# 352 instead of 384 columns for TensorE's U products, and the last 32 dense tokens from gathered rows

## What is computed

```python
comb = (sv[:, :, 0, :, None] + sv[:, :, 1, None, :]).reshape(T, PEER_HEADS, K * K)
cs, ci = lax.top_k(comb, K)
idx = ia * PEER_NKEYS + ib
g = jax.nn.softmax(cs, axis=-1)
a = jnp.einsum('td,thkd->thk', xb, u_tab[eb])          # pre-activation: h . U row
w = gb * jax.nn.gelu(a, approximate=False)
return jnp.einsum('thk,thkd->td', w, v_tab[eb])        # weighted sum of V rows
```

## Time and profile before

| | |
|---|---|
| Runs | 1338.08, 1338.53, 1338.57 us; median 1338.53 |
| Profiled execution | span 1336.4 us, by which it is known here; the runs' median is 2.1 us above it |
| TensorE | busy 1314.3 us (98%) |
| VectorE | busy 1160.9 us (87%) |
| ScalarE | busy 656.3 us (49%) |
| GpSimd | busy 573.2 us (43%) |
| DMA | 384.51 MB, mean 288 GB/s |
| Granted TensorE clock | 0.999 of full speed |

### The profile page before, as it was taken

One profiled execution on the slowest core, in us unless ns is written; L12 is line 12 of the kernel. 1 busy time (PEld: TensorE's weight loads), 2 busy tenths in 40 slices (PEclk: granted clock), 3 DMA queues, 4 the chain that ended last, 5 costly groups with the idle time before them and its releaser, 6 DMA issues.

```text
span 1336.4 us, 23193 instructions
## 1 busy us (share of the span) xinstructions
PE 1314.3 (98%) x7713; PEld 712.3 (53%) x7713; DVE 1160.9 (87%) x2288; ACT 656.3 (49%) x926; POOL 573.2 (43%) x347
## 2 busy tenths in 40 slices
PE   6999999999999999999999999999999999999997
PEld 3554555456666666666655555555544444444444
DVE  8866399999988999999778888899998889888887
ACT  5652555556676767676543333333343334333342
POOL 4741233435643434343336666667653433222202
PEclk9999999999999999999999999999999999999999
DMA  7231322336677999999999999999999999999952
GB/s 297 96 111 64 107 83 85 104 96 188 192 252 238 321 386 381 364 359 379 401 332 357 363 362 362 355 402 390 382 368 384 391 388 388 382 370 371 374 181 105
DMA packets 148796, 384.51 MB, mean 288 GB/s; under 512 B 11776, under 2 KB 71424, under 8 KB 146560
## 3 DMA queue, kind: packets, MB, share of 16 engines
q1 hardware_dynamic: 111872, 249.54, 52.8%
q0 software_dynamic: 36864, 134.23, 25.8%
HBM read 340.74 MB, written 42.99 MB: 287 GB/s over the span
## 4 chain that ended last, share of the span: by engine, by line
PE 98%; DVE 1%; ACT 1%; DMA 0%; issue 0%; DVEq 0%; ACTq 0%
PE bank L696 39%; PE bank L684 16%; PE bank L686 16%; PE bank L685 16%; PE bank L961 2%; PE bank L905 2%; PE bank L903 2%; PE bank L711 2%; PE bank L852 1%; PE bank L610 1%; PE bank L810 1%; DVE stats L1381 0%; PE bank L757 0%; PE bank L734 0%; PE bank L746 0%; PE bank L624 0%
## 5 line engine op out<-in xcount | busy, mean ns | idle before, releaser
L696 PE MATMUL bank<-cut,area 128*128 128x512 f16 x2208 | 482.9, 380 | 0.0
L684 PE MATMUL bank<-hT,cut 128*128 128x384 f16 (+1 forms) x1216 | 407.2, 335 | 0.0
L685 PE MATMUL bank<-hT,cut 128*128 128x384 f16 (+1 forms) x1216 | 407.2, 335 | 0.0
L686 PE MATMUL bank<-hT,cut 128*128 128x384 f16 (+1 forms) x1216 | 407.1, 335 | 0.0
L992 ACT ACTIVATE cut<-raw 128x1024 f16<-128x1024 f32 x246 | 255.7, 1053 | 198.7 <-PE bank L696 130.8
L696 PEld LDWEIGHTS bank<-cut,area 128*128 128x128 f16 x2208 | 215.8, 98 | 256.7
L1358 DVE SCALAR_TENSOR_TENSOR cut<-raw,cut 128x1024 f16<-128x1024 f32 x198 | 250.6, 1267 | 60.6 <-ACT cut L992 59.2
L1207 ACT ACTIVATE gelu_out<-bank 128x384 f32<-128x384 f32 x120 | 58.9, 491 | 252.9 <-PE bank L686 252.9
L592 POOL DMA_INDIRECT ple_sb<-u_rows_dram,expert_id x64 | 112.9, 1764 | 134.0 <-DVE dots_now L1708 101.5
L582 POOL TENSOR_TENSOR cut<-raw,cut 128x1024 f16<-128x1024 f32 x48 | 108.0, 2250 | 139.9 <-ACT cut L1002 139.9
L686 PEld LDWEIGHTS bank<-hT,cut 128*128 128x128 f16 x1216 | 118.8, 98 | 89.0
(11 more groups left out here) (207 smaller groups left out, 1556.7 us busy)
## 6 DMA issues: line engine op xcount, KB each, us to landing
raw<-tiles_dram SPq DMA_DIRECT2D x298, 512.0 KB, 6.5
gates_scratch<-area SPq DMA_DIRECT2D x12, 2048.0 KB, 11.6
area<-gates_scratch SPq DMA_DIRECT2D x32, 768.0 KB, 9.6
gelu_scratch<-gelu_out SPq DMA_DIRECT2D x80, 192.0 KB, 5.1
area<-gelu_scratch SPq DMA_DIRECT2D x20, 768.0 KB, 11.3
norm_rows<-norms_dram SPq DMA_DIRECT2D x3, 1024.0 KB, 7.6
hn<-x_dram SPq DMA_DIRECT2D x4, 512.0 KB, 5.2
out_dram<-hn SPq DMA_DIRECT2D x3, 512.0 KB, 2.6
```

Source lines behind the costliest of these rows:

```text
L684: nc.tensor.matmul(dst, w[0], hT[:, 0, k, 0:width], start=(k == 0), stop=False)
L685: nc.tensor.matmul(dst, w[0], hT[:, 1, k, 0:width], start=False, stop=False)
L686: last = nc.tensor.matmul(dst, w[1], hT[:, 0, k, 0:width], start=False, stop=(k == KD - 1))
L696: mm = nc.tensor.matmul(bank[:, 2 * tt + h, :], lhs(a)[:, tt * P:(tt + 1) * P], cut[:, t.slot, b, h * HALF:(h + 1) * HALF], start=(first a ...
```

## The change

The last 32 of the 384 dense tokens (`TOK` tokens of the third tile, `TU` = 352 up) get their U pre-activations no longer from TensorE. They have 32 x 128 picks; laid over 128 partitions (four groups of 32 tokens with 32 picks each) these are `EXTRA` = 32 gathered blocks of 128 U rows, and as many dots on VectorE with `extra_h`, a copy of h of these 32 tokens in each of the four groups. VectorE transposes the dots in 32 x 32 blocks (`turn_extra`), ScalarE applies the GeLU, VectorE multiplies with the gates (`weigh_extra`) and writes the result into the rows from which the one-hot matrices of these tokens take their values. So the gate matrix holds gate times GeLU for them, and the GeLU columns of these tokens are set to 1. V products stay 384 wide.

The extra 32 dots come first, in the gate stage, so the sparse tokens' dots and sums move back: there the stage's last 16 dots are theirs (as before, one gather and one dot a tile); then 8 in the kept tiles and 24, 24, 24 and now 32 in four eights; the fifth eight has 26 sums and the late part 102 instead of 80, 10 or 11 for an eight. VectorE's loops over the gate stage, the eights and the late part are written out, and the copies `dots_now` and `sparse_w_now`, which the loops needed, are gone.

```diff
+TU = TD - TOK
+EXTRA = TOK * HK // P
+EXTRA_TILE, EXTRA_AT = TU // P, TU % P
 KEPT_DOTS = 8
-EIGHT_DOTS = (24, 24, 24)
-EIGHT_SUMS = (26, 22)
+EIGHT_DOTS = (24, 24, 24, 32)
+EIGHT_SUMS = (26,)
+LATE_SUMS = (10, 10, 10, 10, 10, 10, 10, 10, 11, 11)
...
@@ SP
             sp.dma_start(subkeys_sb, subkeys).then_inc(subkeys_in, 16)
+            sp.wait_ge(norm_done, 2 * TT - 1)
+            for g in range(P // TOK):
+                sp.dma_start(extra_h[g * TOK:(g + 1) * TOK, :],
+                             hn[EXTRA_AT:EXTRA_AT + TOK, EXTRA_TILE, :]).then_inc(extra_h_in, 16)
             for n in range(T_Q + RING, T_Q + LOAD_AHEAD):
...
@@ GpSimd
+            for n, (table, ids, i) in enumerate([*((u_rows, extra_id, i) for i in range(EXTRA)),
+                                                 *((u_rows, expert_id, i) for i in range(HK)),
+                                                 *((v_rows, expert_id, i) for i in range(HK))]):
...
@@ TensorE, all U tiles
-                    columns(Tile(T_U + j, 4, it), u_index + 4 * it + j, j % 2, TD, 6)
+                    columns(Tile(T_U + j, 4, it), u_index + 4 * it + j, j % 2, TU, 6)
...
@@ ScalarE
-                nc.scalar.activation(dst, bank[:, 6 + slot % 2, 0:TD], ACT.Gelu,
+                nc.scalar.activation(dst[:, 0:TU], bank[:, 6 + slot % 2, 0:TU], ACT.Gelu,
...
-            with act.Fori(1, U_GATES // 8 - 1) as it:
+            with act.Fori(1, EXTRA // 8) as it:
                 build_gates(it)
+            act.wait_ge(extra_turned, 1)
+            nc.scalar.activation(extra_w, extra_w, ACT.Gelu).then_inc(extra_gelu, 1)
+            for it in range(EXTRA // 8, U_GATES // 8 - 1):
+                build_gates(it)
+            act.wait_ge(extra_done, 1)
             build_gates(U_GATES // 8 - 1, True)
...
@@ VectorE, before top-k
+            nc.vector.memset(gelu_out[:, :, TU:], 1.0).then_inc(ones_done, 1)
...
@@ VectorE, after top-k
+            for g in range(P // TOK):
+                tokens_at, picks = slice(EXTRA_AT, EXTRA_AT + TOK), slice(g * EXTRA, (g + 1) * EXTRA)
+                own.mark(nc.vector.scalar_tensor_tensor(
+                    out=extra_f[g * TOK:(g + 1) * TOK, :], in0=picked[tokens_at, 0, EXTRA_TILE, picks],
+                    scalar=float(NKEY), in1=picked[tokens_at, 1, EXTRA_TILE, picks], op0=ALU.mult, op1=ALU.add))
+            own.settle()
+            nc.vector.tensor_copy(extra_id, extra_f).then_inc(ids_done, 1)
...
+            nc.vector.memset(gelu_kept[:, :, TU:], 1.0).then_inc(ones_done, 1)
...
@@ VectorE, gate stage
+            def dot(n):
+                dve.wait_ge(rows_in[n % ROW_RING], 16 * (n // ROW_RING + 1))
...
+                values, into = (extra_h, extra_dots[:, n:n + 1]) if n < EXTRA else \
+                    (hn[:, ND, :], dots[:, n - EXTRA:n - EXTRA + 1])
+                nc.vector.tensor_tensor_reduce(slot, slot, values, 1.0, 0.0, ALU.mult, ALU.add,
+                                               into).then_inc(rows_used, 1)
+            def turn_extra():
+                dve.wait_ge(rows_used, EXTRA)
+                nc.vector.transpose(extra_w, extra_dots).then_inc(extra_turned, 1)
+            def weigh_extra():
+                dve.wait_ge(extra_gelu, 1)
+                own.link(nc.vector.tensor_tensor(extra_w, extra_w, extra_gate, ALU.mult))
+                own.link(nc.vector.tensor_copy(rows[:, 2, TU:TD], extra_w))
+                nc.vector.tensor_tensor(rows[:, 3, TU:TD], extra_w, rows[:, 2, TU:TD],
+                                        ALU.subtract).then_inc(extra_done, 1)
...
+                    if 8 * it == EXTRA and s == 0:
+                        weigh_extra()
+            for it in range(U_GATES // 8):
+                if 8 * it == EXTRA:
+                    turn_extra()
+                build_gates(it)
...
@@ VectorE, late part
-                    if not end:
-                        add_row(v, first + 8 * e + v, first // ROW_RING + e + v // ROW_RING, v % ROW_RING)
+                    for a in range(first + count * v // 8, first + count * (v + 1) // 8):
+                        add_row(a)
```

More of the change, by code:

```diff
@@ L273, in layer @@
         staged = part([2, 4, BATCH, 2], F16)
+        extra_h = part([D])
+        extra_f = part([EXTRA])
+        extra_id = part([EXTRA], U32)
+        extra_dots = part([EXTRA])
+        extra_w = part([TOK])
+        extra_gate = part([TOK])
         gelu_out = sb("gelu_out", [P, VG, TD])
@@ L585, in _ @@
             pool.wait_ge(ids_done, 1)
[L586 to L595, removed]
+            for n, (table, ids, i) in enumerate([*((u_rows, extra_id, i) for i in range(EXTRA)),
+                                                 *((u_rows, expert_id, i) for i in range(HK)),
+                                                 *((v_rows, expert_id, i) for i in range(HK))]):
+                if n == 4:
+                    pool.wait_ge(ple_added, ND)
+                    pool.wait_ge(gated, TT)
+                if n == EXTRA:
+                    pool.wait_ge(ids_done, 2)
+                at_least(pool, rows_used, n - ROW_RING + 1)
+                nc.gpsimd.indirect_dma_start(
+                    expert_rows[n % ROW_RING], None, table,
+                    bass.IndirectOffsetOnAxis(ap=ids[:, i:i + 1], axis=0)
+                ).then_inc(rows_in[n % ROW_RING], 16)
             pool.wait_ge(norms_in, 16 * 3)
@@ L1919, in final_bias, with late @@
                                                op1=ALU.add).then_inc(final_done, 1)
-            def late(e):
-                fixed = isinstance(e, int)
-                end = fixed and e == N_LATE // 8 - 1
-                if not end:
-                    weights_now(first + 8 * e, 8)
+            def late(e, first, count):
+                end = e == N_LATE // 8 - 1
                 halves = (slice(0, HALF), slice(HALF, D))
@@ L1939, in late @@
                         final_bias(0, slice(0, D), 2)
-                    if not end:
-                        add_row(v, first + 8 * e + v, first // ROW_RING + e + v // ROW_RING, v % ROW_RING)
-                    t = Tile(T_LATE + 8 * e + v) if fixed else Tile(T_LATE + v, 8, e)
-                    if not fixed or t.n + SPLIT_AHEAD + 1 < T_ALL:
+                    for a in range(first + count * v // 8, first + count * (v + 1) // 8):
+                        add_row(a)
+                    t = Tile(T_LATE + 8 * e + v)
+                    if t.n + SPLIT_AHEAD + 1 < T_ALL:
                         make_late(e, v + 3)
-                    if not fixed or t.n + SPLIT_AHEAD < T_ALL:
+                    if t.n + SPLIT_AHEAD < T_ALL:
                         weight_low(N_BOTH + 8 * e + v + 2, (v + 2) % RING)
                         split_lo(t.plus(SPLIT_AHEAD))
-            before = own.count
-            with dve.Fori(0, N_LATE // 8 - 2) as e:
-                own.turns, own.count = e, before
-                late(e)
-            own.turns, own.count = 0, before + N_LATE // 8 - 2
-            late(N_LATE // 8 - 2)
-            late(N_LATE // 8 - 1)
+            for e, count in enumerate((*LATE_SUMS, 0)):
+                late(e, first, count)
+                first += count
             for i in (1, 2):
```

114 lines of the change are left out of this document (42 added, 72 removed).

## The result

| | before | after |
|---|---|---|
| Runs, median (lowest to highest) | 1338.5 us (1338.1 to 1338.8) | 1344.9 us (1341.6 to 1348.1) |
| Profiled execution, span | 1336.4 us | 1342.7 us |
| TensorE, VectorE busy | 98%, 87% | 96%, 89% |
| DMA | 384.51 MB | 401.87 MB |

The ratio after to before is 1.0049 (95% interval 1.0038 to 1.0060): the change makes the kernel 6.4 us slower. The prediction was 1328, 10 us faster, with a range that ended at 1338: wrong in sign and outside its range.

What follows compares the result with a forecast made beforehand. TensorE was taken to bound the kernel, with VectorE and DMA right behind. 41.0 us saved, less 6.3 in the gate stage and 24.5 behind DMA, gave 10.2: 1338.5 to 1328 us, range 1316 to 1335, with rivals 1307 to 1338.

Steps and rivals of the forecast that it cites:

- 352-column matmul: TensorE's U products: 149.2 ns a matmul instead of 162.5, saving 0.32 us a tile, 41.0 us for 128 tiles.
- cut for U tile 26: End of top-k: VectorE's cut done at 382.9 us, TensorE waiting 1.4 us for it (bounds 0 and 4).
- first one-hots: Start of VectorE's gate-stage one-hot operations: 409.1 us instead of 416.63, 7.5 us earlier (bounds 6 and 8.8).
- bound of the gate stage: 24 pairs of U tiles: VectorE binds at 9.05 us a pair; TensorE leaves at 625.0, gaining 19.3 us.
- At the fourth eight the gain: Start of the fourth product eight: TensorE there at 840.1 us instead of 870.3, 30.2 us earlier.
- DMA moved 173.9 MB against 174.9: Fourth eight on: 32 more blocks, 16.8 MB, on top of 158.1 MB; DMA becomes the bound, full to about 1285 us.
- 24.5 behind DMA (447.5 - 423), which contains the 3.0 of VectorE: Fourth eight to last eight: DMA needs 447.5 us, TensorE 423; the loss includes VectorE's 3.0 us for 32 dots.
- 3 us after DMA was done: End of the late part: 3 us added for cutting the last arrival, so the last eight starts at 1287.6 us.
- After it nothing changes: From the start of the last eight at 1287.6 us to the end, no further gain or loss.
- DMA hidden: Rival for the fourth eight on: DMA never holds TensorE up, gain 31.7 us, 1306.8 us in all; chance 0.20.
- DMA binding in the gate stage: Rival: DMA sets gate-stage pairs at 9.41 us instead of 9.05, 8.6 us more, 1336.9 us in all; chance 0.13.
- loop of the late part's buffers: Rival: late GeLU loads landing x longer cost TensorE 0.5 + x us an eight, ten times; 1352 at x = 4; chance 0.12.

Runs made afterwards that it cites:

- even dots: The changed kernel with 26, 26, 26, 26 dots in the four eights instead of 24, 24, 24, 32: 1338.8 us, ratio 1.0008.
- three rows fewer ahead: The changed kernel with GpSimd at most 5 gathered rows ahead of VectorE instead of 8, from the fifth eight's first V row: 1345.3 us, ratio 1.0041.
- every second V row halved: The changed kernel with every second gathered V row brought as half a row, same number of gathers and sums: 1323.7 us, ratio 0.989.
- half V rows: The changed kernel with all gathered V rows brought as half rows, same number of gathers and sums: 1321.2 us, ratio 0.988.
- thin extra rows: The changed kernel with 24 of the 32 extra gathers bringing 64 bytes a row instead of 4 KB: 1343.6 us, ratio 1.0038.
- 16 tokens: The same change to the kernel before for 16 tokens instead of 32: 368-column U products, 16 extra gathered blocks, twelve small DMAs; 1338.5 us, ratio 1.0001.
- two halves of the change alone: Kernel before with only 352-column U products and GeLU: 1310.3 us; changed kernel with U products 384 wide again, so only the extra work: 1370.3 us.
- shorter lead: The changed kernel with 26 dots in each of four eights and GpSimd at most 5 rows ahead in the late part: 1337.2 us, ratio 1.0001.
- fewer late sums: The changed kernel with 26 dots in each of four eights, and late sums of 11 in six eights, then 9 in four: 1337.1 us, ratio 0.9989.
- narrower GeLU transfers: The changed kernel with 26 dots in each of four eights and gelu_scratch written and read 352 columns wide instead of 384: 1338.9 us, ratio 1.0003.

## Why the prediction was wrong, step by step

**Right.** A 352-column matmul takes 0.149 us. The cut for U tile 26 was done at 384.1 against 382.9, TensorE's wait 2.6 us against 1.4: inside the bounds. The first one-hots: 410.2 against 409.1. VectorE is the bound of the gate stage, at 9.04 us a pair against 9.05, and TensorE leaves it at 625.8 against 625.0, with 18.4 us gained against 19.3. At the fourth eight the gain is 29.3 against 30.2. From 841 to 1298 us DMA moved 173.9 MB against 174.9; the share stayed full until 1284, where the forecast had it end, and late eights take 32.5 us.

**Where 16.6 us went.** At the fourth eight 0.9. From there to the last eight the forecast had a loss of 20.0 and it was 29.5: 9.5. In the last eight 6.1, where the forecast had nothing.

**The fourth and fifth eights.** Ten late eights lose 14.8 us, which is what 32.5 instead of 31.1 us each come to. So the 9.5 us too little were forecast for the fourth and fifth eights: they lost 14.7, and the forecast left 5.2 for them. The term that failed is "24.5 behind DMA (447.5 - 423), which contains the 3.0 of VectorE". It takes DMA as one average over 448.5 us, and VectorE's work as hidden behind it.

- In the fourth eight the loss is 7.2 us. The prediction costed the 32 dots on VectorE (3.0 us) and averaged their gathers. The runs show a burst: one load 21.6 us late, a wait of 7.2 us, then DMA itself at half its share. With even dots the gain stays the same over the fourth eight (28.0 and 28.1 us).
- In the fifth eight the loss is 7.5 us. The prediction put VectorE there at nothing, though it has 26 sums in the place of 22. The runs show that VectorE is the bound: busy 55.2 of 58.1 us, and TensorE loses the same when DMA's share is 0.84. How VectorE enters it matters too: with 24 dots in the eight before (16 in the kept tiles) the wait ahead of the last V tile is 3.1 us instead of 4.3. How much of it would be lost again to a full DMA in the late part, were it saved here, no run shows.

The forecast also let TensorE reach the last eight 3 us after DMA was done. DMA was done at 1284, as forecast, and TensorE came 13.8 us later. Eight rows that stand in the ring ahead of need take 10.8 us at 388 GB/s, an estimate that would fill the gap, but the run with three rows fewer ahead gained nothing, so this reading is not supported.

**"After it nothing changes".** Wrong by 6.1 us. The last eight runs at TensorE's pace only when VectorE comes to it with cuts in hand, and in the kernel after it comes with none. With every second V row halved the same eight takes 31 us, and with two sums fewer in each of the last late eights 34.0.

**The rivals.** DMA hidden: wrong; with half V rows, when it nearly is, the kernel gains 17 us. DMA binding in the gate stage: wrong (thin extra rows). The loop of the late part's buffers had 0.12 for slower, and slower it was. Its formula, 0.5 + x us an eight, gives the measured 1.5 us: the median landing of a GeLU load from 1034 to 1231 us is 11.4 us before and 12.4 after, x = 1.0. But that is luck, for the loop which the trace shows is another. The chain of waits of the kernel after:

```profile
1114.23 8.89 DMA area<-gelu_scratch
1123.12 1.13 DVE cut L1382
1124.25 1.20 DVE ple_gate L1835
1125.45 1.18 issue
...
1127.10 0.55 DVE area L1828
1127.66 1.14 DVE cut L1382
1128.96 0.33 SPq L391
1129.60 0.38 SPq L402
1130.17 9.03 DMA area<-gelu_scratch
```

A GeLU load is issued at 1114.23. VectorE's first product of that group of four tiles starts 12.4 us later, after a wait (the "issue"). Its next cut frees a buffer, SP issues the tile load for it (L391), and only then come the next gates and the next GeLU load, 3.5 us after the product. So one such loop closes for every group of four tiles, not for eight. In nine groups from 1081 to 1228 us the issue came 3.6 us after the product, the product 12.7 us after the issue before it; together these are the 16.3 us that four tiles take. With the median landings, which are a little below the mean:

| kernel | median landing of a GeLU load, us | with 3.6 us | late part |
|---|---|---|---|
| before | 11.4 | 15.0 | at TensorE's pace |
| every second V row halved | 9.9 | 13.5 | at TensorE's pace |
| 16 tokens | 11.6 | 15.2 | at TensorE's pace |
| after | 12.4 | 16.0 | 16.3 us for four tiles |
| even dots | 12.4 | 16.0 | 16.3 us for four tiles |

TensorE needs 15.54 us for four tiles. The loop fits every row, but so do the bytes: 12.6 MB an eight at 386 GB/s are 32.5 us, and the landing grows with what DMA has to do. Whether throughput or the loop's delay binds isn't shown. One experiment could tell and was not made: VectorE is done with a buffer at 1122.6, but the load into it is issued at 1130.17, 7.5 us later, because SP stands at a tile load. An order on SP in which the GeLU load comes before that tile load would take most of this delay out and move the same bytes.

**The rate of DMA.** The kernel after moved 386 GB/s over 312 us at full share. The Trainium skill ("DMA: Bandwidth & Descriptors", Specifications and Bandwidth) has a limit of about 358 GB/s for a core and 425 GB/s measured with one core; the trace agrees with neither and stands between them, as in the kernel before.

**The sum at par.** TensorE saves 1.28 us for each token taken off (41.0/32), and each token needs one gathered block of 0.524 MB, 1.35 us of DMA at 388 GB/s. With DMA at 0.95 to 1.04 of the time from 413 us on, the exchange moves work from one full engine to another. The two halves of the change alone say so: 28.2 us given, 31.8 taken. Even dots, alone or with a shorter lead, fewer late sums or narrower GeLU transfers, and 16 tokens end between 1337.1 and 1338.9 us, and none is told from the kernel before. No version that computes the whole layer beat it.

## What to carry to other kernels

Before work is moved off the bound engine, price it on every resource that is over 95% busy behind it: here 1.28 us of TensorE went for 1.35 us of DMA. When DMA is close to full, ask not when the last byte arrives but how late the next tile is: count bytes for each stage, not for the sum, and look for the stage with the densest gathers. Do the same for every other engine: a stage whose count changes by four sums has to be costed again on VectorE. A stage that runs at pace only because an engine enters it with a lead has to be costed again when that lead is gone.

## What the runs showed of the hardware

- With four gathers issued for each pair of tiles, a load of 0.5 MB took 21.6 us, three times the kernel's median of 7.3 us; DMA moved 394 GB/s meanwhile (869 to 891 us, share 1.04).
- After a wait of 7.2 us TensorE's 352-column matmuls came 0.29 us apart instead of 0.15: 1.2 GHz instead of 2.4. The granted clock is 0.50 from 893 to 897 us, and 16 matmuls (893.27 to 897.94) take 4.7 us instead of 2.4: the stall of 7.2 us costs 9.5. After the wait of 4.3 us in the fifth eight the granted clock is 0.86 from 960 to 972 us, and the tile takes 5.1 us instead of 3.9.
- The kernels that wait for DMA scatter: 1341.6 to 1348.1 us for the kernel after, 1332.6 to 1342.7 for even dots with fewer late sums. The kernel before stays between 1337.9 and 1340.0 us in all its runs.
